# Output projection in eight parts, four of them inside or beside the unit loop, and the second column tile's low part on GpSimd

## The reference

```python
h = x @ w_in[l]                                   # 1024 x 1892
o_a = sliding_window_sink_attn(...)               # 8 heads of 64
o_b = indexer_sparse_attn(...)                    # 4 heads, each query keeps its 64 best keys
o_c = mla_attn(...)                               # 4 heads, from normalised low-rank q and kv
mix = concatenate([o_a, o_b, o_c])                # 512 + 256 + 256 columns
x = layer_norm(ALPHA * x + mix @ w_out[l])        # 1024 x 1024
x = layer_norm(ALPHA * x + moe_ffn(x, ...))
```

## Time and profile before

| | us |
|---|---|
| median of 3 runs | 1287.69 (1286.9 to 1288.01) |
| the profiled execution, its own time | 1294.08 |
| its span, first to last instruction | 1292.3 |
| PE busy in the span | 1161.7 |
| DVE busy | 779.9 |
| ACT busy | 587.0 |
| POOL busy | 112.6 |
| mean granted TensorE clock (share of full) | 0.935 |

### The profile page before, as it was taken

How to read it: one execution, slowest core, us unless ns; L and a number is a source line. 1 busy time by engine, 2 the same in 40 slices (tenths; PEclk the granted TensorE clock), 3 DMA queues, 4 the chain that set the end, 5 groups by cost and what they waited for, 6 DMA issues and landing times.

```text
span 1292.3 us, 17490 instructions
## 1 busy us (share of the span) xinstructions
PE 1161.7 (90%) x7000; PEld 1027.9 (80%) x7000; DVE 779.9 (60%) x948; ACT 587.0 (45%) x710; POOL 112.6 (9%) x191
## 2 busy tenths in 40 slices
PE   4999989997999998897967999996998959999994
PEld 3999989995999997896747787775987748787873
DVE  5345544776444445597355558896596255459984
ACT  2434445733433442355313446773356214347770
POOL 3000011000000000362000000000370000000000
PEclk9999999998999999897777999998997878999997
DMA  8744444454455655241114558994340005558980
GB/s 265 228 143 129 130 129 131 165 209 149 159 176 186 195 181 155 86 139 36 33 33 163 198 193 293 357 357 145 97 162 1 33 33 188 203 197 319 360 296 33
DMA packets 115078, 215.87 MB, mean 167 GB/s; under 512 B 9546, under 2 KB 79178, under 8 KB 115008
## 3 DMA queue, kind: packets, MB, share of 16 engines
q1 hardware_dynamic: 112432, 209.90, 48.4%
q0 software_dynamic: 1424, 4.59, 1.0%
q10 hardware_dynamic: 1152, 0.42, 0.1%
HBM read 213.80 MB, written 1.09 MB: 166 GB/s over the span
## 4 chain that ended last, share of the span: by engine, by line
PE 71%; DVE 15%; ACT 4%; DMA 4%; issue 3%; POOL 2%; SPq 0%; POOLq 0%; DVEq 0%; ACTq 0%
PE ps L788 16%; PE ps L790 16%; PE ps L789 16%; DVE wlo L1652 4%; PE ps L824 3%; PE ps L825 3%; PE ps L826 3%; PE ps L888 3%; ACT whi L1294 2%; PE ps L873 2%; PE ps L856 1%; PE ps L1162 1%; PE ps L1163 1%; PE ps L848 1%; DMA raw<-in_w_in 1%
## 5 line engine op out<-in xcount | busy, mean ns | idle before, releaser
L1652 DVE TENSOR_TENSOR wlo<-raw,whi 128x2048 fp32r<-128x2048 f32 (+2 forms) x175 | 389.9, 2231 | 238.1 <-ACT whi L1294 236.7
L1294 ACT ACTIVATE whi<-raw 128x2048 fp32r<-128x2048 f32 (+2 forms) x175 | 323.5, 1853 | 155.0 <-PE ps L790 92.4
L788 PE MATMUL ps<-act_hi,whi 128*128 128x256 f32 (+1 forms) x784 | 228.2, 291 | 11.6 <-DVE act_lo L1659 11.6
L789 PE MATMUL ps<-act_lo,whi 128*128 128x256 f32 (+1 forms) x784 | 226.2, 289 | 0.0
L790 PE MATMUL ps<-act_hi,wlo 128*128 128x256 f32 (+1 forms) x784 | 226.2, 289 | 0.0
L788 PEld LDWEIGHTS ps<-act_hi,whi 128*128 128x128 f32 (+1 forms) x784 | 151.9, 194 | 17.9 <-DVE act_lo L1659 13.2
L789 PEld LDWEIGHTS ps<-act_lo,whi 128*128 128x128 f32 (+1 forms) x784 | 151.8, 194 | 1.3
L790 PEld LDWEIGHTS ps<-act_hi,wlo 128*128 128x128 f32 (+1 forms) x784 | 151.8, 194 | 1.0
L788 PE MATMUL ps<-whi,moe_r 128*128 128x512 f32 x320 | 128.7, 402 | 1.0 <-DVE wlo L1652 1.0
L789 PE MATMUL ps<-wlo,moe_r 128*128 128x512 f32 x320 | 126.7, 396 | 0.0
L790 PE MATMUL ps<-whi,moe_r 128*128 128x512 f32 x320 | 126.4, 395 | 0.0
(11 more groups left out here) (264 smaller groups left out, 1998.8 us busy)
## 6 DMA issues: line engine op xcount, KB each, us to landing
raw<-in_w_in SPq DMA_DIRECT2D x45, 1024.0 KB, 5.5
raw<-in_w_down SPq DMA_DIRECT2D x35, 1024.0 KB, 5.1
raw<-in_w_gate SPq DMA_DIRECT2D x48, 512.0 KB, 4.6
raw<-in_w_up SPq DMA_DIRECT2D x48, 512.0 KB, 6.3
raw<-in_w_gu SPq DMA_DIRECT2D x22, 1024.0 KB, 5.1
raw<-in_w_out SPq DMA_DIRECT2D x12, 1024.0 KB, 4.9
arena<-in_w_gate SPq DMA_DIRECT2D x16, 512.0 KB, 4.6
arena<-in_w_up SPq DMA_DIRECT2D x16, 512.0 KB, 6.3
```

The source lines that it names most:

```text
L788: pe.matmul(o, ah, bh, start=first, stop=False)
L789: pe.matmul(o, ah, bl, start=False, stop=False)
L1294: act.activation(whi[:, c % 3, 0:n], raw_of(c, v)[:, 0:n], ACT.Copy).then_inc(hi_made, 1)
L1652: dve.tensor_tensor(wlo[:, c % 3, 0:n], raw_of(c, v)[:, 0:n], whi[:, c % 3, 0:n].bitcast(F32), ALU.subtract)\
```

## The change

- The low part of tile 1 of each layer is no longer made by DVE ahead of the residual add. GpSimd makes it (`second_low`), between its `power` for t = 0 and its `power` for t = 1. DVE waits for it before it splits tile 2.
- ACT makes the high part of tile 12 ahead of the unit loop and not in slot 5. DVE makes the low part of tile 11 in slot 1 and not ahead of the loop, and that of tile 12 in slot 6 and not 5.
- The transposes of `mix_tok` are done in two halves of eight (`turn_mix`): columns 0 to 511 in slot 12, the rest after the last output. Their high and low parts follow on ACT and DVE in two halves (`mix_turned`).
- The projection is cut into eight parts of 12 matmuls (`out_part(j, t)`, tile j, token half t). PE order: part (0,0) in slot 14 ahead of the last values product, (1,0) behind it, then the second half of the transposes, (0,1), (1,1), and then (2,0), (3,0), (2,1), (3,1). `early_out` is raised by (3,0), so that 24 matmuls follow it. It uses PSUM banks 0, 1 and 6, 7.
- `WARM` becomes 2, 3, 1, 1, 1, 2 in slots 0, 1, 9, 10, 11, 12; ahead of the loop 4 are issued and not 5. Their operands are rows of `mix_hi`.
- The wait for the last late transpose moves from slot 8 to slot 9.
- The router's sum of a group's two best comes from five short maxima and sums; the ranks of the 32 scores are done behind `one_ready`.

```diff
-WARM = {0: 4, 8: 1, 9: 1, 10: 1, 11: 1, 12: 3, 13: 3, 14: 4}
+MIX_BANK = ((3, 4), (5, 3))
+OUT_BANK = (0, 6)
+WARM = {0: 2, 1: 3, 9: 1, 10: 1, 11: 1, 12: 2}
@@ gpsimd
-            for n in range(2, 6):
+            def second_low(l):
+                c = T_L + 1
+                pool.wait_ge(hi_made, l * 63 + (c + 1))
+                pool.wait_ge(lo_made, l * 63 + c)
+                pool.tensor_tensor(wlo[:, c % 3, :], raw_of(c, l * 21), whi[:, c % 3, :].bitcast(F32), ALU.subtract).then_inc(lo_made, 1)
+            for n in range(2, 5):
                 power(n, n % 2)
+            second_low(0)
+            power(5, 1)
...
-                for t in range(TT):
-                    power(l * 4 + (8 + t), t)
+                power(l * 4 + 8, 0)
+                if l < LAYERS - 1:
+                    second_low(l + 1)
+                power(l * 4 + 9, 1)
@@ tensor
-                keep_warm(3, 5)
+                keep_warm(3, 4)
+                def out_part(j, t):
+                    n = T_L + J_WO + j
+                    tile_ready(n, v)
...
+                    for half in range(2):
+                        d = slice(half * 512, half * 512 + 512)
+                        for k in range(2):
+                            x = three(ps[:, OUT_BANK[t] + half, :], mix_hi[:, 2 * j + k, m], mix_lo[:, 2 * j + k, m],
+                                      wh[:, k, d], wl[:, k, d], j == 0 and k == 0, j == 3 and k == 1)
+                    if t == 1:
+                        x.then_inc(tile_used, 1)
+                    elif j == 3:
+                        x.then_inc(early_out, 1)
...
+                    if i == U_PER + 2:
+                        pe.wait_ge(tr_lo, l * 12 + 14)
+                        out_part(0, 0)
                     if i >= 3:
                         values(unit_layer(i - 3), nu + (i - 3))
+                    if i == U_PER:
+                        pe.wait_ge(o_ready, nu + 6)
+                        turn_mix(0)
+                out_part(1, 0)
                 pe.wait_ge(o_ready, nu + U_PER)
+                turn_mix(1)
+                out_part(0, 1)
+                out_part(1, 1)
+                pe.wait_ge(tr_lo, l * 12 + 16)
                 for t in range(TT):
-                    turn(mix_tok, t)
-                for j in range(4):
-                    pe.wait_ge(tr_lo, l * 12 + 16)
-                    down_tile(T_L + J_WO + j, ...)
+                    out_part(2, t)
+                    out_part(3, t)
@@ scalar
+                split(12)
...
                     if i < U_PER:
                         exps(unit_layer(i), nu + i)
-                    if i == 5:
-                        split(12)
-                turned_hi(l * 3 + 3, mix_hi)
+                    if i == U_PER:
+                        mix_turned(0)
+                mix_turned(1)
@@ vector
-            split_lo(T_L + 1)
...
+                dve.wait_ge(lo_made, v * 3 + (T_L + 2))
                 split(2)
...
                 split(10)
-                split(11)
...
                     if i >= 3:
                         outs(unit_layer(i - 3), nu + (i - 3), lk)
-                    if i == 5:
+                    if i == 1:
+                        split(11)
+                    if i == 6:
                         split(12)
+                    if i == U_PER:
+                        mix_turned(0)
+                mix_turned(1)
...
-                ranks(flat(bi), 8, cnt8)
-                lk(dve.scalar_tensor_tensor(out=flat(sel_b), in0=cnt8, scalar=1.5, in1=flat(bi), op0=ALU.is_lt, op1=ALU.mult))
-                lk(dve.tensor_reduce(gsum, flat(sel_b).rearrange("p (g k) -> p g k", k=4), AX.X, ALU.add))
+                dve.tensor_tensor(top, b4[:, :, :, 0], b4[:, :, :, 1], ALU.max)
+                lk(dve.tensor_tensor(both, b4[:, :, :, 0], b4[:, :, :, 1], ALU.add))
+                dve.tensor_tensor(gsum, top[:, :, 0], top[:, :, 1], ALU.add)
+                lk(dve.tensor_tensor(cntg, both[:, :, 0], both[:, :, 1], ALU.max))
+                lk(dve.tensor_tensor(gsum, gsum, cntg, ALU.max))
                 ranks(gsum, 2, cntg)
                 dve.tensor_scalar(flat(one_g), cntg, 0.5, None, ALU.is_lt).then_inc(one_ready, 1)
                 dve.wait_ge(one_ready, l + 1)
+                ranks(flat(bi), 8, cnt8)
```

More of the change, by code:

```diff
@@ L857, in scores @@
                 x.then_inc(sc_full, 1)
+            idle_rows = mix_hi[:, 8:10, :]
             def keep_warm(bank, n):
                 for _ in range(n):
-                    pe.matmul(ps[:, bank, :].rearrange("p (a b) -> p a b", a=2), act_hi[:, 0, 0:P], act_hi[:, 0:2, :], start=True, stop=True)
+                    pe.matmul(ps[:, bank, :].rearrange("p (a b) -> p a b", a=2), idle_rows[:, 0, 0:P], idle_rows, start=True, stop=True)
             def turn_probs(u, n):
@@ L1539, in _, with mix_turned @@
                 block_out(3, [(one(ak_t), 0, 2)], 6)
+                split(12)
+                def mix_turned(half):
+                    for t in range(TT):
+                        act.wait_ge(tr_full, (l * 3 + 3) * 4 + (2 * half + t + 1))
+                        act.activation(mix_hi[:, 4 * half:4 * half + 4, t * P:(t + 1) * P],
+                                       ps[:, MIX_BANK[half][t], :].rearrange("p (k c) -> p k c", k=4), ACT.Copy).then_inc(tr_hi, 1)
                 nu = l * U_PER + U_L0
```

27 lines of the change are left out of this document (20 added, 7 removed).

## The result

| | before | changed |
|---|---|---|
| median of the runs, us | 1287.85 (4 runs, 1286.9 to 1288.87) | 1252.64 (4 runs, 1251.62 to 1256.37) |
| ratio, 95% interval | | 0.9732 (0.971 to 0.9753): faster |
| profiled execution, us (clock) | 1294.08 (0.935) | 1252.97 (0.953) |

The median fell by 35.2 us, where 41.4 were forecast. The two profiled executions lie 41.1 apart. The sum came out almost to the point there, partly by luck: two of its terms were off, and the step from the profile to the median was wrong.

The account below looks back on a forecast made before the run. The unit loop was taken to be bound by PE at half clock after a gap. Terms -18.9 - 20.6 - 5.5 - 1.6 + 5.2 = -41.4 gave 1252.7 us profiled, 1246 for the median, range 1239 to 1263.

Parts of the forecast that it names:

- slots 0 to 3: Loop start: without tile 11's low part ahead of them on DVE, the first exponentials come sooner, -2.4 us.
- tile 11's return: Tile 11's 2.3 us come back on DVE behind the second logits; taken as 0, bound +2.3.
- rival 2: Clock still falls in part of the loop: slots 8 to 11, 1261 us; slots 2 to 4 only, under 3; chance 0.21.
- slot 7 to 8: Unit loop: without the waits around tile 12's split, slot 8 follows after 2.45 us and not 6.75, -4.3.
- slots 8 to 11: Unit loop: with the gap gone the clock stays high, four slots take 10.4 us and not 17.7, -7.3.
- slot 12 to the projection's last matmul: Loop's end: fewer warm-ups and no 1.89 us wait ahead of the projection, together -4.9 us in layer 0.
- Residual: After the projection: 24 matmuls behind `early_out` let DVE add the first half sooner, -2.75 us in each layer.
- Router: Router on DVE: `one_ready` comes 0.95 us sooner and moved ranks fill a wait, -0.8 us in each layer.
- Second low part: Two entries: DVE's norm waits for POOL's subtraction at the SBUF ports, +2.4 and +2.8, together +5.2 us.
- Rivals 1, 3 and 4: Ports don't meet, 1237 (0.10); clock low from slot 1 to part (0,0), 1283 (0.04); low two parts longer, 1292 (0.03).
- The median: Whole kernel: the profiled execution's gain of 41.4 us is carried over unchanged to the median, giving 1246 us.
- 59 to 61 us a layer: Sign: the loop from first scores to the projection's last matmul takes 59 to 61 us, where it took 79.

Follow-up runs that it names:

- the experiment with 12 matmuls: Changed kernel with the projection's last four parts reordered so that 12 matmuls, not 24, follow `early_out`: 1257.76 us, ratio to before 0.9769.
- the second profile, of 1292.41: The kernel before, unchanged, timed and profiled again: median 1289.80 us over 12 runs, ratio 0.9993; profiled execution 1292.41.

## Why the prediction was right, and where it was off

The forecast of faster held, and the cause that it named (a gap ahead of a loop bound by PE at half speed) is shown by the two halves: with the splits alone moved the low clock of slots 8 to 11 is gone, with them alone put back it is there again. The loop by the forecast's own steps, from the scores of unit 0, PE's starts:

| step | forecast | layer 0 | layer 1 |
|---|---|---|---|
| slots 0 to 3 | -2.4 | -2.75 | -2.95 |
| slots 4 to 6 (tile 11's return, rival 2) | 0, bound +2.3 | +1.18 | +5.59 |
| slot 7 to 8 | -4.3 | -4.34 | -4.32 |
| slots 8 to 11 | -7.3 | -7.72 | -7.74 |
| slot 12 to the projection's last matmul | -4.9, layer 1 -6.6 | -4.80 | -6.44 |
| sum | -18.9, layer 1 -20.6 | -18.43 | -15.86 |

- *Slot 12 to the end*, put together from five small pieces, came within 0.2 us in both layers. The wait ahead of part (0,0) was 0.25, not 0.4.
- *"I take 0, bound +2.3"* for tile 11's return: +1.18 in layer 0, where PE waits 0.48 us for the logits of unit 4.
- *Rival 2* "in slots 2 to 4 only, PE has slack there, and it costs under 3": the fall came at 953 in layer 1, lasted into slot 6 and cost 4.4 us. The failing step is its price. This fall did not end with the gap; it went on for 10.2 us, with PE busy without a pause from 955 on, and in slots 5 and 6 there is no slack. The argument against the rival, "the clock held through slots 3 to 7 with this same work", misread the kernel before. There slot 3 begins at 589.53, and these are its stretches:

```profile
588.00:590.00 2.00, 2.00 (x10) 1.64 (x10) 1.93 (x4) 1.70 (x7) 1.92 (x4) 0.50 0.00 0
590.00:592.00 2.00, 2.00 (x10) 1.31 (x9) 1.48 (x4) 1.76 (x7) 0.69 (x3) 0.50 0.03 8
```

  Three of its four us ran at 0.50, and at that speed PE had no gaps in it. The waits of 0.64 to 0.99 us ahead of the late transposes of slots 2 to 4 at the full clock were new in the changed kernel.
- *Residual* -2.75: -2.72 in each layer, and 2.7 again in the experiment with 12 matmuls.
- *Router* -0.8: from the first instruction on the scores to the first copy of the selection it took 6.64 us and before 7.63, so -1.0. The whole stretch up to the experts' end varies by more than that from one execution to the next.
- *Second low part* +5.2: the ports met as forecast, POOL took 4.51 and 4.49 and DVE stood for 4.16 more. The term is +1.96 + 2.36 = +4.3, since POOL starts a little ahead of DVE. Rivals 1, 3 and 4 fall. That this part of the change costs and does not gain held.
- *The median.* "I take the gain over to the median in us" is the step that failed, by 6 us. The profile of before was of an execution 5 us over the mean of 51, that of the changed kernel of one at its mean. Its clock, 0.935 against a mean of 0.938, says that it had more time at the low clock than the usual one; in which stretches is not shown, since the second profile, of 1292.41, has the same two loops in sum (216.1 us against 216.0). Of the splits' 28, 24.4 came in the loops of their own profile (a fall in layer 1 took its part) and some 21 in the medians.

Of the signs that were to show it, "59 to 61 us a layer" held in layer 0 (60.2) and not in layer 1 (64.7, with the fall).

That the sum of the profile, -41.4 against -41.1, was so near is luck: the fall in layer 1 (+4.4) was made good by the first block (-1.1), the column tiles (-1.9) and the low part (-0.9 against forecast), none of them foreseen. The gain over the mean of many executions is 35.7.

## What to carry to other kernels

Where PE bounds a loop, first look at the granted clock and at the gap that stands ahead of each fall: moving one 2-us copy out of the loop gave 4.3 us a layer by itself and 7.7 by the clock behind it, and idle time of PE that seems free is worth filling with matmuls that nobody reads, also around a norm. Before moving work to GpSimd, list the VectorE instructions beside it that have two tensor inputs in SBUF; idle time of VectorE itself, behind the critical norm, was the better place by 8.3 us over two entries (6 to 7 in the medians, 8 by the ratios). And take several profiles, or the clock of several runs, before a gain read from one execution is carried over to a median.

## What was not expected of the hardware

- The same instructions with the same gaps end in a fall of the clock in one layer and not in the other, and with 0.71 us busy in 2 it stayed where with 0.84 it fell. Once fallen, it stayed at 0.50 for 10.2 us there, most of them with PE busy without a pause; other falls in these loops lasted from 3.4 us (layer 0 with the splits alone moved) to 20.5 (before, behind slot 7, with PE busy 2.00 in 2 from 608 on) and 23.9 (the splits put back). What sets the length is open.
- Executions of one kernel on one chip, one after the other, spread over 10 us (1284.38 to 1294.80), and the mean granted clock goes with it.
- A one-column instruction of VectorE with its inputs in SBUF took 1.98 us beside GpSimd's subtraction and 0.22 without it, while a 1024-column add with one input in PSUM ran through beside it.
